# The last expert pass of a two-layer decoder: 128 columns of the down projection moved behind the scatters

## The reference

```
def swiglu(h, w_gate, w_up, w_down):
    return (jax.nn.silu(h @ w_gate) * (h @ w_up)) @ w_down
...
    logits = (t @ w_router).astype(jnp.float32)
    top_v, top_i = lax.top_k(logits, TOP_K)
    top_p = jax.nn.softmax(top_v, axis=-1)
    combine = jnp.sum(jax.nn.one_hot(top_i, N_EXPERTS, dtype=jnp.float32) * top_p[..., None], axis=1)
    for e in range(N_EXPERTS):
        out = out + combine[:, e:e + 1].astype(t.dtype) * swiglu(t, w_gate[e], w_up[e], w_down[e])
...
            x = x + moe_swiglu(h, moe_router[j], moe_w_gate[j], moe_w_up[j], moe_w_down[j])
    return rms_norm(x, final_norm_g)
```

## Time and profile before

| | us |
|---|---|
| median of 3 runs | 1016.61 (1015.64 to 1018.47) |
| the profiled execution, whole | 1018.14 |
| its span, first to last instruction | 1016.4 |
| TensorE busy | 1001.0 (98%) |
| VectorE busy | 592.1 (58%) |
| ScalarE busy | 401.6 (40%) |
| queue of the loads (q1) | 67.2% of the span, 252.94 MB |

### The profile page before, as it was taken

One profiled execution on the slowest core, in us unless ns is written; L12 is line 12 of the kernel. 1 busy time (PEld: TensorE's weight loads), 2 busy tenths in 40 slices (PEclk: granted clock), 3 DMA queues, 4 the chain that ended last, 5 costly groups with the idle time before them and its releaser, 6 DMA issues.

```text
span 1016.4 us, 22264 instructions
## 1 busy us (share of the span) xinstructions
PE 1001.0 (98%) x9679; PEld 862.9 (85%) x9679; DVE 592.1 (58%) x991; ACT 401.6 (40%) x627; POOL 14.2 (1%) x57
## 2 busy tenths in 40 slices
PE   8999999999999999999999999999999999999995
PEld 8999999999999999999999999996566566566552
DVE  6667766577676565376577755755542542542443
ACT  6735656535444344357356565352102002002012
POOL 3000000000000000000000000000000000000000
PEclk9999999999999999999999999999999999999998
DMA  7443543555555466465435437978999999999993
GB/s 286 160 161 113 190 152 101 186 206 197 172 185 184 143 219 205 153 218 181 152 106 185 156 110 265 384 293 343 396 414 415 410 411 414 413 408 414 414 409 127
DMA packets 56016, 255.40 MB, mean 251 GB/s; under 512 B 6609, under 2 KB 6641, under 8 KB 55922
## 3 DMA queue, kind: packets, MB, share of 16 engines
q1 hardware_dynamic: 55346, 252.94, 67.2%
q10 hardware_dynamic: 576, 1.07, 0.3%
HBM read 252.93 MB, written 1.05 MB: 250 GB/s over the span
## 4 chain that ended last, share of the span: by engine, by line
PE 86%; SPq 6%; DMA 3%; DVE 1%; ACT 1%; issue 1%; DVEq 0%
PE ps L1693 27%; PE ps L1688 17%; PE ps L1689 17%; PE ps L1690 17%; SPq L588 6%; PE ps L1682 2%; PE ps L1684 2%; PE ps L1683 2%; DMA raw<-in_dense 2%; DMA e_ring<-in_experts 2%; PE ps L1898 1%; ACT w_hi L727 0%; DVE w_lo L1047 0%; ACT squared L732 0%; DVE xhat L1330 0%
## 5 line engine op out<-in xcount | busy, mean ns | idle before, releaser
L1047 DVE TENSOR_TENSOR w_lo<-raw,w_hi 128x1536 fp32r<-128x1536 f32 (+2 forms) x156 | 247.6, 1606 | 121.6 <-ACT w_hi L727 121.0
L727 ACT ACTIVATE w_hi<-raw 128x1536 fp32r<-128x1536 f32 (+2 forms) x156 | 209.0, 1362 | 144.5 <-DMA raw<-in_dense 141.7
L1688 PE MATMUL ps<-hT_hi,w_hi 128*128 128x256 f32 (+1 forms) x816 | 232.0, 284 | 2.2 <-DVE hT_lo L1133 1.0
L1689 PE MATMUL ps<-hT_lo,w_hi 128*128 128x256 f32 (+1 forms) x816 | 230.0, 282 | 0.0
L1690 PE MATMUL ps<-hT_hi,w_lo 128*128 128x256 f32 (+1 forms) x816 | 229.2, 281 | 0.0
L1693 PE MATMUL ps<-e_ring,xe 128*32 128x352 f32 (+2 forms) x2520 | 190.5, 459 | 0.0
L1693 PEld LDWEIGHTS ps<-e_ring,xe 128*32 128x32 f32 x2520 | 112.2, 110 | 73.8 <-issue 32.3
L1688 PEld LDWEIGHTS ps<-hT_hi,w_hi 128*128 128x128 f32 (+1 forms) x816 | 152.0, 186 | 5.8 <-issue 2.2
L1689 PEld LDWEIGHTS ps<-hT_lo,w_hi 128*128 128x128 f32 (+1 forms) x816 | 152.3, 187 | 0.5
L1690 PEld LDWEIGHTS ps<-hT_hi,w_lo 128*128 128x128 f32 (+1 forms) x816 | 152.2, 187 | 0.4
L1689 PE MATMUL ps<-h_lo,w_hi 128*128 128x256 f32 x352 | 99.2, 282 | 0.0
(11 more groups left out here) (313 smaller groups left out, 1425.2 us busy)
## 6 DMA issues: line engine op xcount, KB each, us to landing
e_ring<-in_experts SPq DMA_DIRECT2D x126, 704.0 KB, 16.6
raw<-in_dense SPq DMA_DIRECT2D x112, 768.0 KB, 4.3
e_ring<-in_experts SPq DMA_DIRECT2D x88, 512.0 KB, 13.9
raw<-in_dense SPq DMA_DIRECT2D x42, 512.0 KB, 3.5
raw<-in_dense SPq DMA_DIRECT2D x3, 544.0 KB, 4.8
e_ahead<-in_experts SPq DMA_DIRECT2D x2, 704.0 KB, 10.9
raw<-in_dense SPq DMA_DIRECT2D x2, 272.0 KB, 3.8
x<-in_x SPq DMA_DIRECT2D x2, 256.0 KB, 4.1
```

The source lines that it names most:

```text
L727: act.activation(slot(n, "hi", k), slot(n, "raw", k), ACT.Copy).then_inc(hi_done, 1)
L1047: dve.tensor_tensor(slot(n, "lo", k), slot(n, "raw", k), slot(n, "hi", k).bitcast(F32), ALU.subtract).then_inc(lo_done, 1)
L1688: pe.matmul(out, wh, hi, start=first, stop=False, skip_group_check=True)
L1689: pe.matmul(out, wh, lo, start=False, stop=False, skip_group_check=True)
```

## The change

The down projection of the last pass gets a third strip of columns. `LAST_CUT` is 896: half 1 is cut into 384 columns (512 to 895, bank 6) and 128 columns (896 to 1023, bank 4). Row blocks 0 to 7 do 512 + 384 columns and the overflow as they come in. Blocks 8 to 10 do only their 512 columns as they come in; then follow the overflow of the three, then their 384 columns, then the 128 columns of blocks 0 to 2. Now the scatters of half 0 come, in the order high, low, `y2` for each tile, the `y2` products of the last strip, and the scatters of the 384 columns. Behind them stand the 128 columns of blocks 3 to 10 and, after a wait for VectorE's scaling of bank 4 (`last_ready`), two float32 scatters of 128 columns. ScalarE drains bank 5 first, then the overflow, then the 384 columns, now all in the split format. VectorE follows in the same order, adds four pieces, scales bank 4, and adds the two last pieces. The final norm's squares have three pieces instead of two.

```
-LAST_BANKS = ((2, 3), (0, 1))
+LAST_BANKS = ((2, 3), (0, 1), (5, 7))
+LAST_CUT = HALF + 384
-NORM_PIECES = [[], [], [], OCOLS, [(0, HALF), (HALF, HALF)]]
+NORM_PIECES = [[], [], [], OCOLS, [(0, HALF), (HALF, LAST_CUT - HALF), (LAST_CUT, D - LAST_CUT)]]
...
             act.wait_ge(y_filled, last * 2 + 1)
+            weighted(0)
+            act.wait_ge(y_filled, last * 2 + 2)
             weighted_over()
-            act.wait_ge(y_filled, last * 2 + 2)
-            weighted(0)
             act.wait_ge(y_filled, last * 2 + 3)
-            act.activation(ehid[:, 0:HALF], ps[:, 6, :], ACT.Copy, scale=slot_scale[:, 0:1]).then_inc(y_hi_ready, 1)
-            for h in range(2):
+            w = LAST_CUT - HALF
+            act.activation(y_hi[:, HALF:LAST_CUT], ps[:, 6, 0:w], ACT.Copy, scale=slot_scale[:, 0:1]).then_inc(y_hi_ready, 1)
+            for piece in range(3):
...
+            dve.wait_ge(y_hi_ready, last * 4 + 1)
+            rest(0)
             for h in range(2):
-                dve.wait_ge(y_hi_ready, last * 4 + h + 1)
+                dve.wait_ge(y_hi_ready, last * 4 + h + 2)
                 ins = rest_over(h)
             ins.then_inc(y_split, 1)
...
+            dve.wait_ge(y_hi_ready, last * 4 + 4)
+            rest(1, LAST_CUT - HALF)
+            last_rows(0)
+            last_rows(1)
+            dve.wait_ge(y_filled, last * 2 + 4)
+            dve.tensor_scalar(ehid[:, 0:D - LAST_CUT], ps[:, 4, 0:D - LAST_CUT], slot_scale[:, 0:1], None, ALU.mult).then_inc(last_ready, 1)
+            last_rows(2)
...
-            for q in range(DQ - 1):
-                down(q, last)
-            k = FET - 1
-            down_ready(k, last)
-            down_over([k]).then_inc(y_filled, 1)
-            for h in range(2):
-                down_main(k, h)
...
+            w = LAST_CUT - HALF
+            late = FET - 3
+            for q in range(late // 2):
+                for k in k_pair(q):
+                    down_ready(k, last)
+                    if k == TURNED:
+                        pe.wait_ge(turn1_read, last * 2 + 1)
+                    down_main(k, 0)
+                    down_main(k, 1, w=w)
+                if q == TURNED // 2:
+                    pe.wait_ge(turn1_read, last * 2 + 2)
+                down_over(k_pair(q))
+            for k in range(late, FET):
+                down_ready(k, last)
+                down_main(k, 0)
+            down_over(range(late, FET)).then_inc(y_filled, 1)
+            for k in range(late, FET):
+                down_main(k, 1, w=w)
+
+            def down_last(ks):
+
+                for k in ks:
+                    down_main(k, 1, LAST_CUT, D - LAST_CUT, 4)
...
+            down_last(range(3))
             pe.wait_ge(y_split, last * 3 + 5)
             for tt in range(TT):
+                scatter(2 * tt, LAST_BANKS[0][tt])
             for tt in range(TT):
+                out, tokens = last_piece(tt)
+                plain(out, selT[:, 1, tokens], y2[:, 1, w:HALF], stop=False)
+            pe.wait_ge(y_split, last * 3 + 6)
+            for tt in range(TT):
+                scatter(2 * tt + 1, LAST_BANKS[1][tt], w)
+            down_last(range(3, FET))
+            pe.wait_ge(last_ready, 1)
+            for tt in range(TT):
+                out, tokens = last_piece(tt)
+                plain(out, selT[:, 0, tokens].bitcast(F32), ehid[:, 0:D - LAST_CUT], start=False).then_inc(added_filled, 1)
```

More of the change, by code:

```diff
@@ L495, in build @@
         x_gain_ready, row_scale_ready = sem("x_gain_ready"), sem("row_scale_ready")
+        last_ready = sem("last_ready")
         out_ready, out_ready_a, s_out = sem("out_ready"), sem("out_ready_a"), sem("s_out")
@@ L1014, in _ @@
             act.wait_ge(y_filled, last * 2 + 1)
+            weighted(0)
+            act.wait_ge(y_filled, last * 2 + 2)
             weighted_over()
-            act.wait_ge(y_filled, last * 2 + 2)
-            weighted(0)
             act.wait_ge(y_filled, last * 2 + 3)
-            act.activation(ehid[:, 0:HALF], ps[:, 6, :], ACT.Copy, scale=slot_scale[:, 0:1]).then_inc(y_hi_ready, 1)
-            for h in range(2):
+            w = LAST_CUT - HALF
+            act.activation(y_hi[:, HALF:LAST_CUT], ps[:, 6, 0:w], ACT.Copy, scale=slot_scale[:, 0:1]).then_inc(y_hi_ready, 1)
+            for piece in range(3):
                 for tt in range(TT):
-                    act.wait_ge(x_sum, TT * h + tt + 1)
-                    squares(h, tt, 4)
+                    act.wait_ge(x_sum, TT * piece + tt + 1)
+                    squares(piece, tt, 4)
             norm_root(4)
@@ L1599, in turned1, with rest @@
                 turn_over(8, 1, 0, 3).then_inc(turn1_read, 1)
-            def rest(h):
-                cols = slice(h * HALF, (h + 1) * HALF)
-                dve.scalar_tensor_tensor(out=y_lo[:, cols], in0=ps[:, 5 + h, :], scalar=slot_scale[:, 0:1],
+            def rest(h, w=HALF):
+                cols = slice(h * HALF, h * HALF + w)
+                dve.scalar_tensor_tensor(out=y_lo[:, cols], in0=ps[:, 5 + h, 0:w], scalar=slot_scale[:, 0:1],
                                          in1=y_hi[:, cols].bitcast(F32), op0=ALU.mult, op1=ALU.subtract).then_inc(y_split, 1)
@@ L1644, in _, with last_rows @@
             turned1(last)
+            dve.wait_ge(y_hi_ready, last * 4 + 1)
+            rest(0)
             for h in range(2):
-                dve.wait_ge(y_hi_ready, last * 4 + h + 1)
+                dve.wait_ge(y_hi_ready, last * 4 + h + 2)
                 ins = rest_over(h)
             ins.then_inc(y_split, 1)
-            dve.wait_ge(y_hi_ready, last * 4 + 3)
-            rest(0)
-            for h in range(2):
+            def last_rows(piece):
+                c0, w = NORM_PIECES[4][piece]
                 for tt in range(TT):
-                    dve.wait_ge(added_filled, last * 4 + 4 + 2 * h + tt + 1)
-                    xs_ = x[:, tt, h * HALF:(h + 1) * HALF]
-                    dve.tensor_tensor(xs_, ps[:, LAST_BANKS[h][tt], :], xs_, ALU.add).then_inc(x_sum, 1)
+                    dve.wait_ge(added_filled, last * 4 + 4 + 2 * piece + tt + 1)
+                    xs_ = x[:, tt, c0:c0 + w]
+                    dve.tensor_tensor(xs_, ps[:, LAST_BANKS[piece][tt], 0:w], xs_, ALU.add).then_inc(x_sum, 1)
+            dve.wait_ge(y_hi_ready, last * 4 + 4)
[5 more added lines that the diff above has]
+            last_rows(2)
             mean_square(4)
@@ L2039, in gather, with scatter @@
                     ins.then_inc(xe_filled, 1)
-            def scatter(g, bank=None):
+            def scatter(g, bank=None, w=HALF):
                 tt, h = g // 2, g % 2
-                out, tokens, cols = ps[:, 5 + g % 3 if bank is None else bank, :], slice(tt * P, (tt + 1) * P), slice(h * HALF, (h + 1) * HALF)
+                out, tokens, cols = ps[:, 5 + g % 3 if bank is None else bank, 0:w], slice(tt * P, (tt + 1) * P), slice(h * HALF, h * HALF + w)
                 plain(out, selT[:, 0, tokens], y_hi[:, cols], stop=False)
                 plain(out, selT[:, 0, tokens], y_lo[:, cols], start=False, stop=False)
-                plain(out, selT[:, 1, tokens], y2[:, h, :], start=False).then_inc(added_filled, 1)
+                plain(out, selT[:, 1, tokens], y2[:, h, 0:w], start=False).then_inc(added_filled, 1)
             def expert_ready(u, i):
@@ L2103, in down_ready, with down_main @@
                 expert_ready(2 * KQ * 4 + 2 * k, i)
-            def down_main(k, h):
-                cols = slice(h * HALF, (h + 1) * HALF)
-                ins = quads(5 + h, HALF, ehT[:, k, :], [down_unit(k, e)[:, cols] for e in range(2)], k == 0, k == FET - 1)
+            def down_main(k, h, c0=None, w=HALF, bank=None):
+                c0 = h * HALF if c0 is None else c0
+                cols = slice(c0, c0 + w)
+                ins = quads(5 + h if bank is None else bank, w, ehT[:, k, :], [down_unit(k, e)[:, cols] for e in range(2)], k == 0, k == FET - 1)
                 if k == FET - 1:
@@ new lines, in _, with last_piece @@
+            for k in range(late, FET):
[7 more added lines that the diff above has]
+                    down_main(k, 1, LAST_CUT, D - LAST_CUT, 4)
+            def last_piece(tt):
+                return ps[:, LAST_BANKS[2][tt], 0:D - LAST_CUT], slice(tt * P, (tt + 1) * P)
@@ L2202, in _ @@
+            down_last(range(3))
             pe.wait_ge(y_split, last * 3 + 5)
             for tt in range(TT):
-                out, tokens = last_rows(0, tt)
-                plain(out, selT[:, 0, tokens], y_lo[:, 0:HALF], start=False).then_inc(added_filled, 1)
-            pe.wait_ge(y_hi_ready, last * 4 + 4)
+                scatter(2 * tt, LAST_BANKS[0][tt])
             for tt in range(TT):
-                out, tokens = last_rows(1, tt)
-                plain(out, selT[:, 0, tokens].bitcast(F32), ehid[:, 0:HALF], start=False).then_inc(added_filled, 1)
+                out, tokens = last_piece(tt)
+                plain(out, selT[:, 1, tokens], y2[:, 1, w:HALF], stop=False)
```

## The result

The changed kernel takes 1022.27 us (median of 7, 1019.0 to 1023.1); the kernel before, beside it, 1017.80 (median of 7, 1015.64 to 1018.81). The ratio is 1.0036, interval 1.0026 to 1.0045: slower by 2.7 to 4.6 us. A second set, seven executions against thirty of before, gives 1.0041 (1.0026 to 1.0056). The forecast time was 1019.7, the range 1018.0 to 1022.1, the chance of slower 0.58; the medians of before in these sets (1017.80 and 1018.06) lie 1.2 and 1.5 us above the one that the forecast started from, 1016.61. So the measured median lies 0.2 us above the upper end of the range; on the level that the forecast started from, 1016.61 x 1.0036 = 1020.3 us lies inside it.

What follows compares the result with a forecast made beforehand. In the last third weight transfers set the pace, and everything after the last landing is serial. Exposed overflow 1.66 us plus last strip 1.45 us gave +3.1 on a median of 1016.61: 1019.7 us, range 1018.0 to 1022.1.

Steps and rivals of the forecast that it cites:

- overflow copies start: ScalarE's drain of the overflow bank starts at 1002.66, 1.66 us later than before, behind one product and three blocks' overflow.
- first add: VectorE's adds behind the scatter matmuls were to run from 1006.66.
- last add ends: VectorE's adds of the last 128-column strip, 0.33 us each, were to run 1011.36 to 1012.02.
- reduction starts: Reduction of the squares was to start at 1012.46, where it started at 1009.36 before.
- The work left behind the last landing: TensorE work after the last weight block lands: 6.5 us in place of 2.15; 1.66 and 1.45 us exposed.
- The deferred 384 columns: Three blocks' 384 columns, 1.93 us behind the last landing, end before TensorE's wait for the overflow drain; add nothing.
- The middle value for the 384-column group: Cost of a 384-column matmul group on TensorE, taken as 0.32 us, between 0.216 and 0.43.
- Issue bounds the short products: Rival: issue sets the 64 short matmuls of the 128-column strip, 3.0 to 4.0 us, 1.3 to 2.2 more; chance 0.13.
- The clock falls in the gaps: Rival: TensorE's clock halves for some 3 us after thin work at the last transfers; +4.6 us in all; chance 0.17.
- The signs of being wrong: Wrong if the last transfer moves, granted clock reads below 1.00 before 1010, or overflow copies start before 1002.
- The strip hides: Rival: bank 4's 128 columns finish before VectorE's fourth add ends at 1009.2; +1.8 us, 1018.4; chance 0.15.
- The tail: From the reduction of the squares to the end, everything stays the same: 7.04 us.

Runs made afterwards that it cites:

- the kernel with the deferral alone: Kernel before plus one part: blocks 8 to 10 do only 512 columns as they land, then overflow, then other halves; no third strip. Ratio 1.0029.
- the early strip: Changed kernel with the 128 columns of blocks 0 to 9 moved into the two transfer waits, only block 10's behind the scatters. Ratio 1.0013.
- the in-order kernel: Changed kernel with blocks 8 and 9 doing overflow and 384 columns as they land; last strip as in the change. Ratio 1.0021.
- the last version: Nothing deferred, 128 columns of two or three blocks ahead of waits for blocks 7 to 10, four squares; against the kernel before, ratio 1.0001.

## Why the prediction was right, step by step

The forecast was slower, by 3.1 us at full clock, and that is what the second profile shows. The steps, in us after TensorE's restart:

| step | forecast | measured |
|---|---|---|
| overflow copies start | 2.43 | 2.43 |
| overflow drained | 5.38 | 5.38 |
| first add | 6.43 | 6.42 |
| last add ends | 11.79 | 11.76 |
| reduction starts | 12.23 | 12.30 |
| end of the span behind it | 7.04 | 6.80 |

- *The work left behind the last landing* was the right thing to count, and its two exposed parts have the forecast's size: 1.66 for the overflow (1.65 in the kernel with the deferral alone) and 1.45 for the strip. The 1.45 for the strip isn't quite what the early strip gave back, also 1.45: the forecast's figure is net, and its own hidden case left 1.8 - 1.66 = 0.14 of it in place, where 1.72 - 1.65 = 0.07 was measured. So the exposed products were 0.1 us dearer than forecast, and the rest 0.1 cheaper. The deferred 384 columns were rightly put at nothing.
- *The middle value for the 384-column group* (0.32) was right: in the first profile they start 0.32 apart (loads at 1005.03, 1005.35, 1005.67, at full clock).
- *Issue bounds the short products*: no. The row of the changed kernel is 64 matmuls in 1.96 us, 1.7 of it starts, 27 ns each:
```profile
1010.49 1.69 PEld L1706 LDWEIGHTS ps<-e_ring,ehT 128*32 128x32 f32 x64 [0.26 <-issue]
1010.50 1.96 PE L1706 MATMUL ps<-e_ring,ehT 128*32 128x128 f32 x64
```
  The Trainium skill (TensorE: Matmul & The Clock Gate, section "Wait — 56ns, not 53.3ns?") has 62 ns per matmul for one decoding mode; at 27 ns over 64 in a row no such cost shows in this trace.
- *The clock falls in the gaps* had 0.17 and happened in 6 of 14 executions by their mean clock. Its length was guessed as 3 us and measured as 3.4, its price was forecast as 1.5 and measured as 1.54 in D, and its whole, +4.6, as +4.71. The chance was too low. It was worked out as one event that is or isn't; as a thing that strikes a share of the executions it belonged into the sum, with 0.4 x 1.5 = 0.6 us. Over the 14 spans the executions with a low mean clock raise the mean by 1.0 us (1020.05 against 1019.09 for the other eight).
- *The signs of being wrong* that the prediction gave came up in the first profile: the clock read 0.55 long before 1010. They fit its own rival on the clock and not its sum. The last transfer moved too (1000.62 and 999.18), but one way and the other with the same kernel, so the edit isn't the cause.
- *The strip hides* had 0.15; it would have needed half-cost products, which the row above rules out.
- *The tail* was forecast as unchanged and is 0.23 us shorter in the changed kernel and in all its relatives but the deferral-only kernel. The difference is a gap that the kernel before has between VectorE's reciprocal and the next step (idle 0.27 us against 0.03). Why was not settled.

The forecast time of 1019.7 lay 2.6 us below the measured median: 1.2 of it in the level of before, the rest in the clock and in the spread of seven executions. How it divides between these two isn't shown: in that set only two of the seven have 0.996, and the median execution has 0.998.

## What to carry to other kernels

Where the last transfer sets the end, every product that could run ahead of it and is put behind it costs its full length, unless an engine that ends later covers it: count the work left at the last landing, not the total. TensorE's idle time in front of a transfer isn't worthless either: if work is taken out of it, the clock can fall, and here it fell just when the deferred work came. A reordering that looks neutral in busy time should be tried with the wait filled, and judged by several executions, not by one profile; their mean clock helps, but a fall can hide in it.

## What was not expected of the hardware

- The clock also fell from TensorE's wait of 1.90 us at the drain followed by scatters (D of the in-order kernel, 0.50 from 1006.7 on), while the one profile of the kernel before, with a wait of 1.35 us at the same point, held 1.00. Its 30 further executions have a mean of 0.997 or 0.998, which doesn't rule such a fall out.
- Six idle products in each of two waits, 1.60 us of pure extra work each time, and every one of 11 executions had 0.997 or more.
- The last landing varied from 998.1 to 1001.1 us over the profiles, with the same 252.94 MB of weights in all of them (the sets ran on different chips, and the earliest landing, of the last version, may owe something to that). That is about as much as the whole change costs. Such a spread would go a long way to explain why most intervals of the ratios are some 2 us wide; it was not measured on the unprofiled executions.
